# Placing the weight slabs that stream past the normed input 64 bytes to one side

## The reference, cut to what matters

```python
proj = rmsnorm(h, norm_mix[0]) @ w_in_a           # retention: q, k, v, g, 6144 columns
h = h + (silu(g) * o) @ w_out_a
h = h + (silu(xn @ w_gate) * (xn @ w_up)) @ w_down # dense, 2816 wide
h = h + (p @ w_ple_up) * sigmoid(rmsnorm(h, g) @ w_ple_gate)
kv = rmsnorm(h, norm_kv) @ w_kv                    # band attention: k, v, and q from another norm
y = y + gates[e] * swiglu(xn, w_gate[e], w_up[e], w_down[e])   # 8 experts, top 2
...
for l in range(2):                                 # second block
    (sq, ..., g_hg) = split(rms_norm(x, norm_mix) @ w_in[l])
    x = x + (sigmoid(g_sb)*y_sb + sigmoid(g_dsa)*y_dsa + sigmoid(g_hg)*y_hg) @ w_out[l]
    x = x + square(relu(rms_norm(x, norm_mlp[l]) @ w_up[l])) @ w_down[l]
```

## Time and profile before

| | us |
|---|---|
| median of 3 runs | 2577.74 |
| lowest and highest of them | 2577.26, 2581.29 |
| the profiled execution, its own time | 2583.29 |
| span of the profiled execution | 2581.5 |

### The profile page before, as it was taken

One profiled execution on the slowest core, in us unless ns is written; L12 is line 12 of the kernel. 1 busy time (PEld: TensorE's weight loads), 2 busy tenths in 40 slices (PEclk: granted clock), 3 DMA queues, 4 the chain that ended last, 5 costly groups with the idle time before them and its releaser, 6 DMA issues.

```text
span 2581.5 us, 32667 instructions
## 1 busy us (share of the span) xinstructions
PE 2504.0 (97%) x13495; PEld 2123.7 (82%) x13495; DVE 1901.5 (74%) x2001; ACT 1462.2 (57%) x1358; POOL 0.2 (0%) x4
## 2 busy tenths in 40 slices
PE   8999999999999999999999999999999999999999
PEld 7978997867888888888888887797779988776898
DVE  5656657448989898988988888766876567687655
ACT  5444335545767676767676766647544444664433
POOL 0000000000000000000000000000000000000000
PEclk9999999998999999999999999999999999999999
DMA  7544754328999898989899995343235544422553
GB/s 263 184 145 163 231 190 147 131 103 336 371 346 365 342 369 337 371 339 372 339 359 345 355 357 202 127 164 131 89 127 192 183 174 167 144 98 98 182 194 131
DMA packets 89252, 597.59 MB, mean 231 GB/s; under 512 B 11425, under 2 KB 15889, under 8 KB 18065
## 3 DMA queue, kind: packets, MB, share of 16 engines
q1 hardware_dynamic: 89104, 595.50, 62.0%
HBM read 594.41 MB, written 1.05 MB: 231 GB/s over the span
## 4 chain that ended last, share of the span: by engine, by line
PE 86%; DVE 8%; ACT 4%; DMA 1%; issue 1%; SPq 0%; DVEq 0%; ACTq 0%
PE ps L213 84%; DVE ring_rounded L990 2%; ACT high_rounded L977 1%; DVE arena_rounded L2513 1%; PE ps L2229 1%; DMA ring<-in_slabs 1%; DMA const<-in_consts 0%; PE ps L754 0%; ACT arena L1749 0%; ACT arena L1774 0%; PE ps L1729 0%; DVE arena L3141 0%; DVE arena L3298 0%; DVE arena L3303 0%; DVE arena L2558 0%
## 5 line engine op out<-in xcount | busy, mean ns | idle before, releaser
L213 PE MATMUL ps<-high_rounded,arena_rounded 128*128 128x512 f32 x2768 | 865.4, 394 | 6.3 <-DVE arena_rounded L2513 2.6
L990 DVE TENSOR_TENSOR ring_rounded<-ring,high_rounded 128x2048 fp32r<-128x2048 f32 (+2 forms) x227 | 512.2, 2265 | 268.1 <-ACT high_rounded L977 267.2
L213 PEld LDWEIGHTS ps<-high_rounded,arena_rounded 128*128 128x128 f32 x2768 | 514.9, 189 | 117.8 <-DVE arena_rounded L2513 6.0
L977 ACT ACTIVATE high_rounded<-ring 128x2048 fp32r<-128x2048 f32 (+2 forms) x227 | 428.7, 1892 | 303.5 <-PE ps L213 279.9
L213 PE MATMUL ps<-ring_rounded,arena_rounded 128*128 128x512 f32 x1000 | 391.7, 392 | 0.0
L213 PE MATMUL ps<-xT_high_rounded,high_rounded 128*128 128x256 f32 x1280 | 360.0, 281 | 3.4 <-DVE xT_rounded L819 2.3
L213 PE MATMUL ps<-xT_high_rounded,ring_rounded 128*128 128x256 f32 x1280 | 358.0, 280 | 0.0
L213 PE MATMUL ps<-xT_rounded,high_rounded 128*128 128x256 f32 x1280 | 358.0, 280 | 0.0
L213 PE MATMUL ps<-arena_rounded 128*128 128x512 f32 x928 | 355.0, 392 | 2.4 <-DVE arena_rounded L2532 2.3
L2513 DVE TENSOR_TENSOR arena_rounded<-arena,high_rounded 128x2048 fp32r<-128x2048 f32 x136 | 309.1, 2287 | 30.7 <-ACT high_rounded L2295 30.7
L2295 ACT ACTIVATE high_rounded<-arena 128x2048 fp32r<-128x2048 f32 x136 | 259.0, 1916 | 65.7 <-PE ps L213 65.6
(11 more groups left out here) (331 smaller groups left out, 2938.5 us busy)
## 6 DMA issues: line engine op xcount, KB each, us to landing
ring<-in_slabs SPq DMA_DIRECT2D x219, 1024.0 KB, 4.8
arena<-in_w_down_moe SPq DMA_DIRECT2D x88, 1024.0 KB, 4.9
arena<-in_w_up_moe SPq DMA_DIRECT2D x72, 1024.0 KB, 5.0
ring<-in_w_gate_moe SPq DMA_DIRECT2D x56, 1024.0 KB, 4.9
arena<-in_w_gate_moe SPq DMA_DIRECT2D x56, 1024.0 KB, 4.8
ring<-in_w_up_moe SPq DMA_DIRECT2D x40, 1024.0 KB, 4.8
ring<-in_w_down_moe SPq DMA_DIRECT2D x24, 1024.0 KB, 4.8
ring<-in_slabs SPq DMA_DIRECT2D x4, 912.0 KB, 4.5
```

Of the source, the lines that this page charges most:

```text
L213: return self.pe.matmul(out, lhsT, rhs, start=start, stop=stop, skip_group_check=True)
L977: act.activation(as_rounded(m, m.highs[n % HIGHS][:, 0:size]), m.slots[n % RING][:, 0:size], ACT.Copy).then_inc(m.rounded, 1)
L990: dve.tensor_tensor(as_rounded(m, slot), slot, as_rounded(m, m.highs[n % HIGHS][:, 0:size]), ALU.subtract).then_inc(m.slabs_split, 1)
```

## The change

`ring` and `high` grow by 16 floats (64 bytes) for each place. Each place now has two possible starts, 64 bytes apart: `m.slots` and `m.highs` on one side, `m.slots_off` and `m.highs_off` on the other. The side alternates with the number of the place, since a place's room is 8256 bytes and not a multiple of 128. Wide slabs (`chunks == 4`) and `2.out` use the `_off` starts for their load, their rounding, the subtraction and the matmuls; all other slabs and the experts use the first ones. No instruction is added or removed. `arena` and what follows it start 512 bytes later.

```diff
@@ class TensorSide: slab
-        return as_rounded(self.m, shaped(self.m.highs[n % HIGHS])), as_rounded(self.m, shaped(self.m.slots[n % RING]))
+        return as_rounded(self.m, shaped(high_of(self.m, n))), as_rounded(self.m, shaped(slot_of(self.m, n)))
@@ class Slab
+    @property
+    def beside_normed(self):
+        return self.chunks == 4 or self.name == "2.out"
@@
+BLOCK = 16
@@ place
-    m.ring = split_sb("ring", [P, RING, SLAB])
-    m.high = split_sb("high", [P, HIGHS, SLAB])
+    m.ring = split_sb("ring", [P, RING * (SLAB + BLOCK)])
+    m.high = split_sb("high", [P, HIGHS * (SLAB + BLOCK)])
...
-    m.highs = [m.high[:, i, :] for i in range(HIGHS)]
-    m.slots = [m.ring[:, i, :] for i in range(RING)]
+    places = [(m.ring, i) for i in range(RING)] + [(m.high, i) for i in range(HIGHS)]
+    by_side = []
+    for side in range(2):
+        at = [i * (SLAB + BLOCK) + BLOCK * ((n + side) % 2) for n, (_, i) in enumerate(places)]
+        by_side.append([flat[:, a:a + SLAB] for (flat, _), a in zip(places, at)])
+    m.slots, m.highs = by_side[0][:RING], by_side[0][RING:]
+    m.slots_off, m.highs_off = by_side[1][:RING], by_side[1][RING:]
@@ scalar_split
-        act.activation(as_rounded(m, m.highs[n % HIGHS][:, 0:size]), m.slots[n % RING][:, 0:size],
+        act.activation(as_rounded(m, high_of(m, n)[:, 0:size]), slot_of(m, n)[:, 0:size],
@@ vector_lows
-        slot = m.slots[n % RING][:, 0:size]
+        slot = slot_of(m, n)[:, 0:size]
...
-                          as_rounded(m, m.highs[n % HIGHS][:, 0:size]), ALU.subtract).then_inc(
+                          as_rounded(m, high_of(m, n)[:, 0:size]), ALU.subtract).then_inc(
@@
+def slot_of(m, n):
+    return (m.slots_off if m.stream[n].beside_normed else m.slots)[n % RING]
+
+def high_of(m, n):
+    return (m.highs_off if m.stream[n].beside_normed else m.highs)[n % HIGHS]
@@ sync_experts, sync_stream
-        sp.dma_start(m.slots[n % RING][:, 0:size], m.w["slabs"][n, :, 0:size]).then_inc(m.landed[n % RING], 16)
+        sp.dma_start(slot_of(m, n)[:, 0:size], m.w["slabs"][n, :, 0:size]).then_inc(m.landed[n % RING], 16)
```

## The result

The changed kernel takes 2589.7 us (median; 2586.0 to 2594.1) where the kernel before took 2580.2 in the same series (2577.3 to 2586.2). The ratio is 1.0034, with a 95% interval of 1.0025 to 1.0043: slower by a third of a per cent, about 9 us. The forecast was 2574.2 with 2571.0 to 2579.5 and a chance of 0.08 for slower. It was wrong in sign. The profiled execution has a span of 2592.3 us and a time of its own of 2594.1.

The account below looks back on a forecast made before the run. TensorE's matmul pitch was taken to bound the kernel. A gain of 3.8 us less 0.3 given back at waits made -3.5 us, from 2577.7 to 2574.2 us, range 2571.0 to 2579.5.

Parts of the forecast that it names:

- The pitch as the place to look: TensorE, matmuls covering 97% of the span: the change could act only through the pitch of some matmuls.
- The period of 128 bytes: Wide slabs and 2.out: agreeing with xT modulo 128 gives 226.7 ns instead of 228.9; all other pairs stay unchanged.
- The third of the joined pieces: Joined slabs, 456 columns: a piece agreeing modulo 128 but 128 off modulo 256, at 203 ns, taken as support for 128.
- the longer period: Rival, chance 0.09: period above 128 bytes, so 2645 ring and high matmuls pay 2.2 ns, 5.8 us; 2583 to 2588 us.
- nothing happens: Rival, chance 0.12: the 2.2 ns on wide slabs and 2.out has another cause that follows xT; 2577.7 us.
- The gain of 3.8 us: Wide slabs and 2.out: 1728 matmuls of 512 columns, each 2.2 ns faster, 3.8 us less.
- Tall slabs unaffected, with two sides for r.qk: Tall slabs costed at 0; r.qk could lose 1.7 us, or 2.hqf could gain as much.
- r.qk at 117.8 gives back 1.7 us: Rival, chance 0.25: r.qk's 384 matmuls take the slow pace behind the new wide stage, 1.7 us more; 2575.9 us.
- The rule weighed: Skill text that loading weights steals no read bandwidth from the running matmul; by it no placement matters, sum 0.
- The closing sentence of the forecast: Stages counted as untouched: a changed pace would make it wrong; 3840 tall matmuls by 4.5 ns are 17 us.

Follow-up runs that it names:

- wide64: Kernel before with slots 8704 bytes apart, wide slabs and 2.out starting 64 bytes later, final norm's gain left out; 2585.8 us (one execution).
- wide192: Kernel before with slots 8704 bytes apart, wide slabs and 2.out starting 192 bytes later, final norm's gain left out; 2577.9 us, ratio 0.9998.
- first_side: Changed kernel's slots 8256 bytes apart kept, but wide slabs and 2.out use the first side like all others; 2587.9 us, ratio 1.0039 to the kernel before.
- x_moved: Kernel before with xT moved to the arena's residue modulo 256, slots 8448 bytes apart, tall slabs 64 bytes in; 2577.6 us, ratio 0.9998.
- arena128: Kernel before with the arena, and nothing ahead of it, moved by 128 bytes; 2584.6 us (one execution).

## Why the prediction was wrong, step by step

**The pitch as the place to look: right.** No wait, load or rounding changed; the loads still take 4.8 us, the subtraction 2266 ns. TensorE's pitch carries 8.8 of the 10.5 us between the traces, and the distance of two addresses sets it, as the forecast had it.

**The period of 128 bytes: this step failed.** "Modulo 128 the wide slabs and 2.out thus come to agree with their stationary operand, and all other pairs stay as they were." For 512 columns the period is 256. Wide slabs at distance 128 run at 232.7 and not at 226.7 ns (wide64), and the other pairs did not stay: two of five ring slots and two of three high slots lie 128 bytes off the arena modulo 256.

**The evidence for it: misread.** The third of the joined pieces, 128 off modulo 256, took 203 ns, "just what the rows stage has". The fourth piece, 32 off modulo 128, took the same 0.61 us, so the forecast's own rows didn't tie that pace to agreement. The joined slabs' mean is 206.5 ns before and after, and 205.7 and 207.0 with wide slabs shifted by 64 and 192 bytes, while the 512-column matmuls beside them go to a mean of 232.5 and of 227.6: the opposite direction. Piece by piece, those that lie 128 off are the quickest: the third in the kernel before, mostly 203 ns, and the first with a shift of 64 bytes, 204 to 205 where no pause falls in. So 456 columns follow another rule than 512, which no run isolated, and their pitch could not be carried over. It was also the argument against the longer period and against "nothing happens", so it set two chances.

**The price of the longer period: mechanism right, size off.** The rival held that 2645 matmuls would pay 2.2 ns, 5.8 us, and named 512 bytes. At distance 128 the price is 6.6 ns if the low half is off and 2.2 if only the high half is. By the slots of ring and high halves, 6 of 15 slabs have the low half off and 6 the high half alone: 0.4 x 6.6 + 0.4 x 2.2 = 3.5 ns on average, 5.3 us for the 1495 of rows; measured 2.9 ns, 4.3 us. Experts pay 1.6 ns on all 4005, since part of their slabs lie in the arena itself and are at distance 0 anyway: 6.4 us. The rival's range, 2583 to 2588, came nearest to 2589.7.

**The gain of 3.8 us: not made.** It would have been at distance 0, as wide192 shows (226.5 ns). The change put wide slabs at distances of 0 and 128, and their mean rose from 229.2 to 230.9. first_side, without the move, has 231.3, 0.4 ns more.

**Tall slabs unaffected, with two sides for r.qk: wrong in the forecast.** The rival "r.qk at 117.8 gives back 1.7 us" is what wide192 and x_moved did; in the changed kernel r.qk stayed at 113.3 but for its first slab. That the wide slabs hand the pace over isn't shown: in arena128 they run at 228.9 as before, no operand of wide or tall slabs has moved, and r.qk runs at 117.8. In the changed kernel the mixed slots took 1.2 ns off each of 3802 tall matmuls, 4.7 us, which hid a third of the loss. The closing sentence of the forecast named tall slabs as the largest thing that could go otherwise; they did, the other way.

**The rule weighed.** The Trainium skill, TensorE: Matmul & The Clock Gate, Part 2, has it that loading the next weights doesn't take read bandwidth from the running matmul. The forecast took that to mean that no placement can matter. These traces show 226.7, 228.9 and 233.3 ns for one shape, and ratios from 0.9953 to 1.0039 from placement alone. Whether the weight load has a part in it, no run shows.

**What stays open.** Why at distance 192 for both halves a tall stage settles at 113.3 or at 117.8 ns. There is one trace of each kernel, so whether a stage keeps its pace from one execution to the next wasn't seen either. Behind rows slabs at 226.7 it was mostly the slow pace, behind those at 233 mostly the fast one, but in arena128 r.qk ran at 117.8 behind wide slabs of 228.9. Nor was it tried why one order of the mixture is fast and the other slow, or what the 1.0 ns between the mean and the steady pace of rows slabs is.

## What to carry to other kernels

Before slots get a new spacing, list for every pair of operands the distance of their addresses, modulo 256 at least, and not only for the pair that the change is for: here 1728 matmuls were aimed at, and the slots of 3768 matmuls with the arena and of 3840 tall ones were moved with them. Take a period from steady runs of many matmuls at each distance, from one kernel that steps through them, before costing anything by it. And where a stage has two paces at one placement, a local gain of 1% can be lost next door; look for the placement that holds the fast pace in every stage, which was here worth 8 us by itself and 12 with xT moved. Before two single traces are set against each other, compare their granted clocks: in arena128 they made 7 us of difference, more than half of what the paces had left.

## What the runs showed of the hardware that was not expected

- A 512-column fp32r matmul takes 226.7, 228.9, 232 to 233 and 233.3 ns when the moving operand lies 0, 64, 128 and 192 bytes past the stationary one modulo 256; xT and the arena as stationary tensor give the same within 0.7 ns.
- At 128 bytes the low half's place decides (233.3 ns), the high half's alone costs little (228.9).
- A 256-column one takes 119.9 ns at distance 0, 118.7 at 128, and 113.3 or 117.8 at 64 and 192. High half at 192 with low half at 64 gives 113.3 in every long stage past xT; the reverse gives 118.9 in most.
- Two paces at the same addresses last through 384 matmuls (r.qk at 113.3 before and 117.8 in arena128).
- Behind the same wait of 2.30 us one execution fell to 1.2 GHz (427 ns a matmul) and another stayed at 2.4 (233 ns). Executions of the kernel before took 2575.7 us on the mean at a granted clock of 0.995 and 2578.3 at 0.993.
